# The output projection of a hybrid encoder layer, two row tiles at a time in seven half-size products in place of eight

## What is computed

```
h    = rms_norm(x)
z    = h @ w_in                      # one projection, columns shared out to the head groups
fox  = forgetting_attention(...) * silu(gate)     # 8 heads x 64   -> 512 columns
ssm  = s5_state_space(...)       * silu(gate)     #                -> 256 columns
mem  = memory_attention(...)     * silu(gate)     # 4 heads x 64   -> 256 columns
y    = x + concat([fox, ssm, mem]) @ w_out        # (2176 x 1024) @ (1024 x 1024)
```

## Time and profile before

| | |
|---|---|
| median of 3 runs | 1517.81 us (1517.54 to 1517.82) |
| the profiled execution's own time | 1520.35 us |
| its span, first to last instruction | 1518.6 us |
| granted TensorE clock, mean | 0.997 of full |
| first matmul of the output projection | 1311.40 us |
| start of the last one | 1512.81 us |

### The profile page before, as it was taken

The page is one execution under the profiler, slowest core; times in us unless marked ns, Lnnn a source line. Parts: engine busy times, 40 slices in busy tenths (PEclk is TensorE's granted clock), DMA queues, the critical chain, the costliest instruction groups (busy, mean ns, idle before and its releaser), DMA issues.

```text
span 1518.6 us, 28650 instructions
## 1 busy us (share of the span) xinstructions
PE 1449.4 (95%) x10318; PEld 1193.6 (79%) x10318; DVE 860.4 (57%) x1873; ACT 713.6 (47%) x1726; POOL 212.8 (14%) x294
## 2 busy tenths in 40 slices
PE   7999999999999989999999999999999999999998
PEld 7998767788777767777777787878878787788886
DVE  3689754772566776564426666666666666322221
ACT  5666422422533553453336666666666668310000
POOL 1111433100143332120001000000000004111110
PEclk9999999999999999999999999999999999999999
DMA  7776699985288696879957736063360602354442
GB/s 213 245 265 215 223 250 244 315 258 176 86 220 304 199 262 220 264 238 322 329 191 161 218 72 141 12 143 80 68 147 12 137 2 69 104 179 157 156 165 99
DMA packets 208140, 271.86 MB, mean 179 GB/s; under 512 B 73536, under 2 KB 147680, under 8 KB 204512
## 3 DMA queue, kind: packets, MB, share of 16 engines
q1 hardware_dynamic: 206960, 270.02, 61.3%
q10 hardware_dynamic: 1040, 0.00, 0.0%
HBM read 184.83 MB, written 83.90 MB: 177 GB/s over the span
## 4 chain that ended last, share of the span: by engine, by line
PE 54%; DVE 6%; issue 5%; ACT 3%; SPq 2%; POOL 2%; DMA 1%; ACTq 0%; DVEq 0%; POOLq 0%
PE attn_s L2331 13%; PE in_g L921 12%; PE attn_pv L2298 10%; PE attn_t L2282 6%; PE attn_s L2263 4%; PE attn_s L2266 3%; DVE attn_tops L2450 2%; ACT attn_probs L2364 2%; PE in_b L1096 1%; POOL in_hv L1793 1%; DMA in_xu<-scratch_xt 1%; DVE attn_probs_turned L2463 1%; PE in_b L1048 1%; PE attn_s L2317 1%; SPq L772 1%
## 5 line engine op out<-in xcount | busy, mean ns | idle before, releaser
L921 PE MATMUL in_g<-in_wh,in_xh 128*128 128x512 f32 (+2 forms) x904 | 333.1, 382 | 11.8 <-DVE in_z L1532 5.4
L921 PE MATMUL in_g<-in_wl,in_xh 128*128 128x512 f32 (+2 forms) x904 | 322.9, 370 | 0.0
L2450 DVE TENSOR_REDUCE attn_tops<-attn_s 128x1 f32<-128x512 f32 (+3 forms) x288 | 172.9, 619 | 129.1 <-PE attn_s L2266 128.9
L2364 ACT ACTIVATE attn_probs<-attn_s,attn_negmax 128x512 f32<-128x512 f32 (+3 forms) x384 | 227.6, 605 | 33.3 <-DVE attn_negmax L2454 33.1
L921 PE MATMUL in_g<-in_wh,in_xl 128*128 128x512 f32 (+2 forms) x904 | 236.4, 380 | 1.4 <-DVE in_xl L1515 1.3
L921 PEld LDWEIGHTS in_g<-in_wh,in_xh 128*128 128x128 f32 x904 | 166.3, 190 | 48.2 <-issue 17.1
L2282 PE MATMUL attn_t<-all_ident,attn_probs 128*128 128x128 f32 x1216 | 189.5, 274 | 7.5 <-ACT attn_probs_turned L2374 5.0
L921 PEld LDWEIGHTS in_g<-in_wl,in_xh 128*128 128x128 f32 x904 | 166.3, 190 | 28.2
L921 PEld LDWEIGHTS in_g<-in_wh,in_xl 128*128 128x128 f32 x904 | 159.3, 191 | 34.9 <-issue 5.3
L2282 PEld LDWEIGHTS attn_t<-all_ident,attn_probs 128*128 128x128 f32 x1216 | 146.0, 141 | 41.6 <-ACT attn_probs L2364 10.4
L2298 PE MATMUL attn_pv<-attn_probs_turned,attn_v 128*64 128x128 f32 x2176 | 134.6, 275 | 0.7 <-DVE attn_out L2487 0.7
(11 more groups left out here) (288 smaller groups left out, 2286.0 us busy)
## 6 DMA issues: line engine op xcount, KB each, us to landing
in_xu<-scratch_xt SPq DMA_DIRECT2D x87, 512.0 KB, 5.4
in_xl<-scratch_xt SPq DMA_DIRECT2D x34, 512.0 KB, 4.6
in_raw<-in_w_in SPq DMA_DIRECT2D x40, 256.0 KB, 5.7
scratch_xt<-in_xu SPq DMA_DIRECT2D x19, 512.0 KB, 5.3
scratch_xt<-in_xl SPq DMA_DIRECT2D x17, 512.0 KB, 6.2
scratch_k<-in_x_turned SPq DMA_DIRECT2D x17, 512.0 KB, 7.4
scratch_q<-in_x_turned SPq DMA_DIRECT2D x17, 512.0 KB, 5.4
in_x_turned<-in_x_prompt SPq DMA_DIRECT2D x16, 512.0 KB, 4.5
```

Of the source, the lines that this page charges most:

```text
L921: last = X.matmul(g_ps[b][:, 0:m], x, ws[:, c, w0:w0 + m], start=(c == 0 and h == 0 and ws is wh), stop=(c == KC - 1 and h == 1))
L2364: last = F(probs[:, s % 2, i, at:at + n, :], s_ps[g % RING][:, at:at + n, :], ACT.Exp, bias=negmax[:, s % 2, top:top + 1], accum_out=total)
L2450: V.tensor_reduce(tops[:, s % 2, i:i + 1], bank[:, 0:n, :].rearrange("p n k -> p (n k)"), AX.X, ALU.max).then_inc(s_top, 1)
```

## The change

The sample tile is done as before, but in four products of 12 matmuls (its columns' second half as A11 (B12 - B11) added to A11 B11 in the x sum, plus A12 B22). The 16 prompt tiles are taken as 8 pairs. In a pair, A11 and A12 are the fox half and the ssm+mem half (512 inner columns each) of the upper tile, A21 and A22 of the lower tile; B11 to B22 are the quarters of `w_out`, 512x512 each. Then

```diff
+PAIR = (("a", "A11", "B11"), ("b", "S2", "T2"), ("c", "S1", "T1"), ("a", "A12", "B21"), ("d", "S3", "T3"),
+        ("c", "S4", "B22"), ("d", "A22", "T4"))
...
+    for q in range(1, PAIRS + 1):
+        more = q < PAIRS
+        order += [("product", q, 0), ("part", q), ("product", q, 1), ("sum", q, 0), ("product", q, 2), ("sum", q, 1)]
+        order += [("product", q, 3), ("y", q, 0)]
+        if more:
+            order += [("mix", 2 * q + 1), ("middle", 2 * q + 1), ("halves", q + 1, "A11")]
+        order += [("product", q, 4), ("y", q, 1), ("sum", q, 2)]
+        if more:
+            order += [("mix", 2 * q + 2), ("middle", 2 * q + 2), ("raw", q + 1, 0), ("raw", q + 1, 1), ("halves", q + 1, "S2"),
+                      ("raw", q + 1, 2), ("raw", q + 1, 3), ("halves", q + 1, "S1"), ("halves", q + 1, "A12")]
+        order += [("product", q, 5), ("y", q, 2)]
+        if more:
+            order += [("halves", q + 1, "S3"), ("halves", q + 1, "S4")]
+        order += [("product", q, 6), ("y", q, 3)]
+        if more:
+            order.append(("halves", q + 1, "A22"))
```

```diff
+            for q in range(1, PAIRS + 1):
+                x = x_in[q % 2]
+                pool.wait_ge(s_xin[q % 2], 16 * (q // 2 + 1))
+                pool.wait_ge(s_part, q)
+                G.tensor_tensor(x[:, 0, 0:512], x[:, 0, 0:512], part, ALU.add).then_inc(s_add, 1)
+                pool.wait_ge(s_sum, sums_upto(q, 0))
+                G.tensor_tensor(x[:, 1, 0:512], x[:, 1, 0:512], u_sum[:, :], ALU.add).then_inc(s_add, 1)
+                pool.wait_ge(s_sum, sums_upto(q, 1))
+                G.tensor_tensor(x[:, 1, 512:], x[:, 1, 512:], v_sum[:, :], ALU.add).then_inc(s_add, 1)
+                G.tensor_tensor(x[:, 0, 512:], x[:, 0, 512:], v_sum[:, :], ALU.add).then_inc(s_add, 1)
+                if q + 2 <= PAIRS:
+                    gated(2 * q + 3)
+                    gated(2 * q + 4)
```

```diff
         if first < n <= first + KC:
             order.append(("w_split", n - first - 1, 1))
+        if first + KC < n <= first + KC + 2:
+            order.append(("t_split", n - first - KC - 1))
...
         if n == len(rounds) + 1:
-            order.append(("mix", 0))
-            order.append(("mixed", 0))
+            order += [("mix", 0), ("middle", 0), ("halves", 0, "A11"), ("halves", 0, "A12")]
         if n == len(rounds) + 2:
-            order.append(("product", 0, 0))
-            order.append(("mix", 1))
-    order += [("mixed", 1), ("product", 0, 1), ("y", 0, 0), ("y", 0, 1)]
...
+            order += [("t_split", 2), ("t_split", 3), ("product", 0, 0), ("product", 0, 1), ("first_sum", 0), ("mix", 1)]
+
+    order += [("middle", 1), ("halves", 1, "A11"), ("product", 0, 2), ("y", 0, 0), ("mix", 2), ("middle", 2)]
+    order += [("raw", 1, 0), ("raw", 1, 1), ("halves", 1, "S2"), ("raw", 1, 2), ("raw", 1, 3), ("halves", 1, "S1")]
+    order += [("t_split", 4), ("t_split", 5), ("product", 0, 3), ("y", 0, 1)]
+    order += [("halves", 1, k) for k in ("A12", "S3", "S4", "A22")]
...
+            for i in range(2):
+                sum_low(i)
+            for o in range(3):
+                gated(o)
+            for i in range(2, 6):
+                sum_low(i)
+            for o in range(3, 5):
+                gated(o)
```

What TensorE waits for ahead of a product of pair q (beside the low part of its left operand):

```diff
+                    if q and j == 0:
+                        pe.wait_ge(s_y, y_upto(q - 1, 0))
...
+                    if q > 1 and j == 2:
+                        pe.wait_ge(s_y, y_upto(q - 1, 2))
+                    if q and j == 3:
+                        pe.wait_ge(s_part, q)
...
+                    if q and j == 5:
+                        pe.wait_ge(s_sum, sums_upto(q, 1))
+                    if q and j == 6:
+                        pe.wait_ge(s_y, y_upto(q, 1))
+                        pe.wait_ge(s_sum, sums_upto(q, 2))
```

More of the change, by code:

```diff
@@ L2031, in attention_and_output @@
             w_lo = Place(nc, same, "attn", K.place).sb("w_lo", [P, KC, D_MODEL], F32R)
-        w_raw, s_w = a.sb("w_raw", [P, KC, D_MODEL]), [a.sem(f"w{c}") for c in range(KC)]
+        w_raw, s_w = a.sb("w_raw", [P, KC, D_MODEL]), [a.sem(f"w{c}") for c in range(HALF)]
+        with ExitStack() as same:
+            t2_lo = Place(nc, same, "attn", K.place).sb("t2_lo", [P, HALF, 512], F32R)
+        t2_raw, sums_raw = a.sb("t2_raw", [P, HALF, 512]), a.sb("sums_raw", [P, 3, 512])
+        stage = sums_raw[:, 0:2, :]
         t_ps = [a.ps(f"t{i}", [P, 4, P]) for i in range(TURNS)]
@@ L2064, in attention_and_output, with place_of @@
         s_yst = K.s_yst
-        s_mix, s_xt, s_mh, s_ml = (a.sem(k) for k in ("mix", "mix_turned", "mh", "ml"))
-        s_g, s_y = ([a.sem(f"{k}{i}") for i in range(2)] for k in ("g", "y"))
+        s_mix, s_xt, s_middle, s_raw, s_hi, s_lo = (a.sem(k) for k in ("mix", "mix_turned", "middle", "raw", "hi", "lo"))
+        s_g, s_y, s_part, s_sum, s_add = (a.sem(k) for k in ("g", "y", "part", "sum", "add"))
         TAIL = first_group[FOX_HEADS - 1]
-        SOURCES = ((0, 4), (6, 8), (4, 6))
         def tile_of(o):
             return o - 1 if o else PROMPT_TILES
+        def place_of(o):
+            return (o + 1) % 2 if o else 0, (o + 1) // 2
         def tail_group(t):
@@ L2203, in sync_program @@
                 store(sp, head - 2)
+                if head - 2 < HALF:
+                    sp.wait_ge(s_t, 4 * (head - 1))
+                    for k in range(2):
+                        sp.dma_start(D.t34[k, head - 2], stage[:, k, :]).then_inc(s_t_out, 16)
             store(sp, FOX_HEADS - 2)
@@ new lines, in tensor_steps @@
+                    if q and j == 6:
+                        pe.wait_ge(s_y, y_upto(q, 1))
+                        pe.wait_ge(s_sum, sums_upto(q, 2))
+                    begins, ends = (q, j) != (0, 3), (q, j) != (0, 1)
+                    for c in range(HALF):
+                        wh, wl = right[weights](c)
+                        for k, (ms, ws) in enumerate(((hi, wh), (lo, wh), (hi, wl))):
+                            last = X.matmul(y_ps[at], ms[left][:, c, :], ws, start=(begins and c == 0 and k == 0),
+                                            stop=(ends and c == HALF - 1 and k == 2))
@@ L2335, in scalar_begin @@
+                    last.then_inc(s_g, 1)
         def scalar_begin(act):
@@ new lines, in vector_steps @@
+                if what == "halves":
+                    q, name = s, rest[0]
+                    dve.wait_ge(s_hi, halves_upto(q, name))
+                    V.tensor_tensor(lo[name], xt_ps[0][:, :, :] if name == "A11" else raw[name], fl(hi[name]), ALU.subtract)\
+                        .then_inc(s_lo, 1)
+                if what == "first_sum":
+                    dve.wait_ge(s_g, products_upto(0, 0))
+                    dve.wait_ge(s_xin[0], 16)
+                    for h in range(2):
+                        x = x_in[0][:, 0, h * 512:(h + 1) * 512]
+                        V.tensor_tensor(x, y_ps["a"], x, ALU.add).then_inc(s_sum, 1)
```

356 lines of the change are left out of this document (268 added, 88 removed).

## The result

| | before | after |
|---|---|---|
| median of the runs | 1517.82 us (4 runs) | 1502.01 us (1499.68 to 1505.14, 4 runs) |
| ratio, 95% interval | | 0.9903 [0.9888, 0.9918] |
| profiled execution, own time | 1520.35 us | 1505.14 us |
| its span | 1518.6 us | 1503.4 us |
| first score matmul of the attention | 799.74 us | 797.66 us |

Faster by 1.0%, where 1.4% was forecast (1496.5 us). Of the 15.2 us between the spans, 2.1 arise before the attention, in code that the change doesn't touch: that point lay anywhere from 793 to 800 us in the profiles of this study. The attention, first score to first product, is 0.9 us longer (511.66 to 512.59), the output stage, first product to last y, 13.5 shorter (201.84 to 188.38), and the end behind the last y 0.6 shorter (5.36 to 4.77).

What follows compares the result with a forecast made beforehand. TensorE was taken to bound the output stage, never waiting. -22.5 + 1.0 - 0.6 = -22.1 us; with the median 2.5 us below the profiled execution 1495.7, plus 0.8 for small terms: 1496.5 us, 8 in 10 range 1493.5 to 1502.5.

Steps and rivals of the forecast that it cites:

- if the stage's saving is under 20 us: Sign that the forecast is wrong; the output stage was to take 179 us in place of 201.6.
- Step 1: Output stage matmuls: 96 fewer at an unchanged 0.2343 us each, -22.5 us; the 26 more products taken at 0.
- Steps 2 and 3: Engine sums and chains inside a pair: TensorE stays the bound at 21.0 us a pair, no stall, 0 us.
- the sum above takes 0: GpSimd and VectorE holding each other up over SBUF reads at the start of the pairs: counted as 0 us.
- rival A: GpSimd's low parts delay VectorE's S1 in pair 1; product 2 stalls 2 to 3 us once: 1499.5 us, chance 0.28.
- Step 4: End of the attention, ScalarE: first split of T2 delays TensorE, +1.0 us; second split hidden, 0, at most 1.0.
- Steps 5 to 7: GpSimd's tile 0 gates just in time, 0 to 1 us; tile 2's loads 0; attention's additions and stores 0, at most 1.
- step 6: T3 and T4 load ahead of tile 2; its gates end 2 us before its mix, 0 us; +7 at 200 GB/s.
- Step 8: End of the kernel: last store has 256 KB in place of 512 KB, -0.6 us, ends 0 and -0.9.
- B: Stall in each of 8 pairs, from bank d or SyncE's waits, 0.5 to 2 us each: 1501 to 1512 us, chance 0.10.
- C: GpSimd's additions behind gates waiting for loads; gain gone at 17 us after issue, 1521 us at 18; chance 0.03.

Runs made afterwards that it cites:

- the last version: Changed kernel with y, S1's low part early, T4's low parts on VectorE, T2's splits after the attention, plus tile 2's loads ahead of T3 and T4: 1493.88 us.
- the one with the eighth product: Changed kernel with y and S1's low part early, T4's low parts on VectorE, plus each pair's last product done twice: 1516.91 us, 0.9992 of before.
- the second execution: The changed kernel run again without any edit: 1504.76 us, 0.9910 of the kernel before.
- a later version: Changed kernel with the sample tile's last y and S1's low part early, T4's two low parts moved from GpSimd to VectorE: 1495.11 us, 0.9852 of before.
- the run with memsets: Changed kernel with GpSimd's low parts of T3 and T4 replaced by memsets and left out of the products: 1494.26 us, 0.9850 of before.
- the kernel with the operands in order of need: Changed kernel with pair 1's operands and the sample tile's last y reordered as the products ask for them: 1500.77 us, 0.9884 of before.

## Why the prediction was right in part and wrong in size

By its own sign ("if the stage's saving is under 20 us") the forecast was wrong: the stage saved 13.5 us.

**Step 1, right.** 96 matmuls fewer, with the same steps: 0.22 to 0.24 us both before and after. -22.5 us was the forecast; the changed kernel's stage without its hole is 22.7 shorter (201.84 to 179.1), and the four stages without a hole of over 0.3 us ahead of a product are 178.5 to 179.5 (not counting the last version, and the one with the eighth product). The eighth product put back confirms it. No cost of the 26 more products is seen.

**Steps 2 and 3, right for pairs 2 to 8.** No idle time of TensorE there; a pair every 20.87 us (V is made at 1466.69 and at 1487.56), forecast 21.0:

```profile
1466.69 0.69 DVE L2810 TENSOR_TENSOR attn_v_sum<-attn_s,attn_u_sum 128x512 f32<-128x512 f32 x1 [2.12 <-PE attn_s L2521]
...
1487.56 0.69 DVE L2810 TENSOR_TENSOR attn_v_sum<-attn_s,attn_u_sum 128x512 f32<-128x512 f32 x1 [2.12 <-PE attn_s L2521]
```

The hold-up of the earlier trace rows is there too: an S4 low part of 1.78 us at 1459.60, where GpSimd's gates run. It is covered, as said.

**Where it failed: "the sum above takes 0"**, the step on GpSimd and VectorE at once, together with rival A. Three mistakes, of different weight:
- The price of the hold-up was worked out in rival A and then set at 0 in the sum, since the row showed GpSimd as the one that waits. At that tile VectorE's operation and GpSimd's had begun together; in the changed kernel VectorE's step begins behind a running low part and waits for up to 2.2 us. Rival A's own number was good: the low part of S1 "near 1333", measured 1330.61 + 1.76 = 1332.4.
- The victim was the wrong one. Rival A named product 2, which asks for S1, and gave 3 us. I had followed the operands of pair 1 and not the banks: product 1 writes bank b, the last y of the sample tile has to read it first, and that y stands in VectorE's list behind all four stretched steps. So the stall began one product earlier and lasted 6.9 us. For the pairs in the steady state I had checked such bank waits; for the first pair, whose list is written out by hand in another order, I had not. Moving this y alone leaves rival A as written (3.2 us at product 2). So rival A's 1499.5 us (1498 to 1502) comes close to the measured 1502.0 in part by luck: it had the cause and the price of a step right, the product that waits and the length of the wait wrong.
- And a hole of this length has a second price, which no term had: the matmuls behind it ran at the lower clock, 2.4 us more for 12 of them at 0.43 us (1.6 in the second execution).

6.9 + 2.4 = 9.3 us, the missing part of the stage: it was to save 22.5 us (to 179.3) and took 188.4, 9.0 more, the later pairs having run 0.1 us each faster than forecast. The span was to be 1496.5 us and was 1503.4, 6.9 more: these 9.0, less the 2.1 by which the attention began earlier in this execution. The medians are 1502.0 against 1496.5, 5.5 us apart. That they are nearer than the stage's miss is luck, since no term of the forecast has the earlier start.

**Step 4, right:** +1.0 forecast for the first split of T2, +0.9 measured, and gone when the splits move. ScalarE's copy took 1.05 us, forecast 1.04. The second split was hidden, as said.

**Steps 5 to 7, right, with less to spare in step 6 than said:** the mix of tile 0 had no wait, that of tile 2 waited 0.2 us in the changed kernel and up to 0.8 in a later version. The preparation during the attention cost nothing.

**Step 8, right:** -0.6 forecast, -0.6 measured.

**The other rivals.** B (a stall in every pair) and C (GpSimd's loop behind the loads, the slow side) did not come: in the run with memsets, GpSimd was so late in pair 1 that VectorE waited 4.2 us for its addition, and TensorE still did not. That the loads would have to be 14 us late for a loss was not tried.

## What to carry to other kernels

When a steady loop has been checked, check the first round on its own: its list is in another order, and each TensorE product waits for its operands and for whoever still has to read its bank, and that reader may stand behind unrelated work in an engine's list. Put the step that frees a bank as early as its own input allows, and ask this of every engine's list, not only of the one that showed the wait. Where VectorE makes things from two SBUF operands on a path that TensorE waits for, keep GpSimd's long operations that read SBUF out of that time, or let one operand come from PSUM (such steps took 0.69 us here; no run timed one that was moved there).

## What was not expected of the hardware

- VectorE's 128x512 step with two SBUF operands took 0.69 us alone or beside GpSimd's memsets, and up to 2.9 us beside GpSimd's 128x1024 subtractions (2.36 us alone, 2.6 beside VectorE). The starts and ends fit with the engines taking turns, whole instructions at a time: the third low part ends about where the held-up step's own 0.69 us can begin. Both engines were slowed.
- After 6.9 us without matmuls the next 12 ran at steps of 0.43 us in one execution and seven in the other (2.4 and 1.6 us lost). After a gap of 3.3 us (3.57 us between starts) seven did too, and 1.6 us were lost; there the granted clock was still 1.00 in the first microsecond after the gap and fell to 0.58 in the next. After 4.5 us, in the kernel with the operands in order of need, 2.2 us were lost. So what is lost behind a gap did not follow its length. A gap of 1.4 us (the last run's) left the clock at 1.00.
